# Last 16 tokens of a chunked scan as one stacked 128-row unit, and two output-gate tiles moved from the tail into the carries

## The reference

```python
def step(S, inp):
    r_t, w_t, k_t, v_t, kk_t, a_t = inp
    sa = jnp.einsum('bhvk,bhk->bhv', S, kk_t)
    S = (S * w_t[:, :, None, :]
         - sa[..., None] * (kk_t * a_t)[:, :, None, :]
         + v_t[..., None] * k_t[:, :, None, :])
    return S, jnp.einsum('bhvk,bhk->bhv', S, r_t)
...
o = ((o - mean) * lax.rsqrt(var + GN_EPS)).reshape(B, T, RWKV_WIDTH) * gn_g + gn_b
o = (o + bonus.reshape(B, T, RWKV_WIDTH)) * g
...
gate_a, gate_b = jnp.split(jax.nn.sigmoid(gate_logits), N_BRANCH, axis=-1)
h = h + (gate_a * y_a + gate_b * y_b) @ w_o[l]
```

## Time and profile before

| | us |
|---|---|
| median of 3 runs | 1664.49 (1661.36 to 1671.22) |
| profiled execution | 1663.75 |
| span of the profiled execution | 1661.8 |
| carry before the second recurrence, first F matmul to first step | 665.77 to 674.10 |
| second recurrence, first step to last matmul between the steps | 674.10 to 709.27 |
| head sums to first branch tile | 714.03 to 753.01 |

### The profile page before, as it was taken

How to read it: one execution, slowest core, us unless ns; L and a number is a source line. 1 busy time by engine, 2 the same in 40 slices (tenths; PEclk the granted TensorE clock), 3 DMA queues, 4 the chain that set the end, 5 groups by cost and what they waited for, 6 DMA issues and landing times.

```text
span 1661.8 us, 32663 instructions
## 1 busy us (share of the span) xinstructions
PE 1559.3 (94%) x11824; PEld 1420.6 (85%) x11824; DVE 1087.2 (65%) x1794; ACT 826.2 (50%) x1425; POOL 379.5 (23%) x168
## 2 busy tenths in 40 slices
PE   5998879999688989898999999999999999999998
PEld 4975569999678988788999999999999888888886
DVE  3424557777668777565549898799999544444444
ACT  3434545555355522134455566667666444444444
POOL 1210112222113200011224324322122222222222
PEclk8995899999789988689999999999999999999999
DMA  6630125556324400024545555544444466666654
GB/s 229 235 119 0 39 78 176 178 188 184 95 89 140 152 2 2 3 84 145 177 139 180 176 177 179 178 148 130 140 137 139 155 188 188 189 189 189 188 187 142
DMA packets 66233, 234.89 MB, mean 141 GB/s; under 512 B 8200, under 2 KB 9240, under 8 KB 66160
## 3 DMA queue, kind: packets, MB, share of 16 engines
q1 hardware_dynamic: 65760, 232.31, 44.9%
q0 software_dynamic: 400, 1.59, 0.3%
HBM read 232.80 MB, written 1.06 MB: 141 GB/s over the span
## 4 chain that ended last, share of the span: by engine, by line
PE 80%; issue 9%; DVE 5%; ACT 3%; POOL 2%; DMA 0%; SPq 0%; DVEq 0%; ACTq 0%; POOLq 0%
PE psum L671 40%; PE psum L1286 21%; PE psum L685 4%; PE psum L1252 3%; PE psum L996 2%; POOL w_lo L513 1%; DVE big L1546 1%; PE psum L659 1%; PE psum L1080 1%; PE psum L791 1%; PE psum L836 1%; PE psum L729 1%; PE psum L1085 1%; PE psum L809 1%; DVE big L1646 1%
## 5 line engine op out<-in xcount | busy, mean ns | idle before, releaser
L671 PE MATMUL psum<-x_hi,w_hi 128*128 128x256 f32 (+1 forms) x2192 | 634.7, 290 | 37.3 <-DVE x_lo L1341 16.5
L671 PE MATMUL psum<-x_lo,w_hi 128*128 128x256 f32 (+1 forms) x2192 | 625.0, 285 | 0.0
L671 PE MATMUL psum<-x_hi,w_lo 128*128 128x256 f32 (+1 forms) x2192 | 621.2, 283 | 0.0
L513 POOL TENSOR_TENSOR w_lo<-ring,w_hi 128x1024 fp32r<-128x1024 f32 x141 | 349.0, 2475 | 1163.7 <-ACT w_hi L499 1163.7
L499 ACT ACTIVATE w_hi<-ring 128x1024 fp32r<-128x1024 f32 x424 | 445.4, 1050 | 92.4 <-PE psum L671 80.2
L671 PEld LDWEIGHTS psum<-x_hi,w_hi 128*128 128x128 f32 x2192 | 417.9, 191 | 47.4 <-issue 31.6
L513 DVE TENSOR_TENSOR w_lo<-ring,w_hi 128x1024 fp32r<-128x1024 f32 x283 | 352.9, 1248 | 157.3 <-ACT w_hi L499 153.9
L671 PEld LDWEIGHTS psum<-x_hi,w_lo 128*128 128x128 f32 x2192 | 420.8, 192 | 0.0
L671 PEld LDWEIGHTS psum<-x_lo,w_hi 128*128 128x128 f32 x2192 | 418.9, 191 | 1.6 <-issue 1.4
L1971 DVE TENSOR_TENSOR h_lo<-big,h_hi 128x256 fp32r<-128x256 f32 x128 | 69.2, 541 | 163.1 <-ACT h_hi L2360 163.1
L1286 PE MATMUL psum<-w_hi,h_hi 128*128 128x512 f32 x512 | 160.8, 395 | 0.0
(11 more groups left out here) (284 smaller groups left out, 1763.4 us busy)
## 6 DMA issues: line engine op xcount, KB each, us to landing
ring<-experts SPq DMA_DIRECT2D x256, 512.0 KB, 3.6
ring<-w_ffn SPq DMA_DIRECT2D x66, 512.0 KB, 3.6
ring<-w_in SPq DMA_DIRECT2D x46, 512.0 KB, 3.6
ring<-w_mid SPq DMA_DIRECT2D x24, 512.0 KB, 3.6
ring<-w_out SPq DMA_DIRECT2D x16, 512.0 KB, 3.9
ring<-w_q SPq DMA_DIRECT2D x16, 512.0 KB, 4.0
big<-w_cmp SPq DMA_DIRECT2D x8, 512.0 KB, 5.6
big<-bias_rows POOLq DMA_DIRECT2D x1, 1536.0 KB, 8.5
```

What stands on the lines that cost most here:

```text
L513: eng.tensor_tensor(w_lo[:, n % RING, :], ring[:, n % RING, :], w_hi[:, n % RING, :].bitcast(F32), ALU.subtract).then_inc(low_ready2 if n ...
L671: mm = pe.matmul(dst, w[:, slot, k * P:(k + 1) * P], x[:, k, t0:t0 + width], start=(n == 0), stop=(n == 3 * len(chunks) - 1))
```

## The change

Group 2 gets code of its own. The 8 heads times 16 tokens are stacked into one block of 128 rows: the upper 64 rows hold the even heads, the lower 64 the odd ones (`side(0)`, `side(1)`), and a gram is one 64x64 matmul to a side, of which the mask keeps the blocks of one head with itself. The blocks off the two sides are zeroed once, and a product, power or application is then one 128-row matmul for all heads. Its effects stand inside the last step. ACT packs four features into `rms` before the scan. Two gate tiles, 8 and 9, are taken out of the tail: in each carry, half of a tile's matmuls follow `carry_values(0)` and half follow `carry_values(1)`. Their sigmoids go to rows of `z2` that are free by then. The splits of tiles 10 to 12 (high) and 10 (low) move into the scan, and those of the tail move up by two.

```diff
+        HOLE_BANK = (7, 5)
+        gate_row = lambda g: 12 + g if g in (8, 9) else g
-        LAST = {"turn": 6, "lt": (3, 5), "l": (3, 5), "qr": (3, 5), "mv": (7, 3), "l2": (7, 3), "l2t": (7, 3), "app0": (4, 5),
...
+        LAST = {"turn": 6, "grams": 3, "mv": 4, "l2": 5, "l2t": 7, "app0": 6, "l4": 5, "l4t": 7, "app1": 4, "l8t": 3, "app2": 6,
+                "app3": 4, "e": 5, "o": 7}
+        stack_gram = lambda a: gram[0][:, a, 0, :]
+        stack_y = ycol[0][:, 0, :]
...
+            def gate_part(g, bank, n0, n1):
+                slot = tile_split(pe, B_MID + g)
+                for n in range(n0, n1):
+                    k = n // 3
+                    w, x = ((w_hi, x_hi), (w_hi, x_lo), (w_lo, x_hi))[n % 3]
+                    mm = pe.matmul(psum[:, bank, 0:TX], w[:, slot, k * P:(k + 1) * P], x[:, k, N_META:T2],
+                                   start=(n == 0), stop=(n == 23))
+                if n1 == 24:
+                    mm.then_inc(tiles_used, 1)
...
+            def stack_grams():
+                kinds = ((S_BETA, alpha), (S_KAPPA, alpha), (S_ALPHA, beta), (S_BETA, rho), (S_KAPPA, rho))
+                for k, (a, b) in enumerate(kinds):
+                    for x in range(2):
+                        mm = pe.matmul(psum[side(x), LAST["grams"], k * HD:(k + 1) * HD], stack_in[side(x), a, :], b[side(x), :, T_LAST],
+                                       start=True, stop=True)
+                mm.then_inc(gram_sum[0], 1)
+            def stack_product(name, a, rhs):
+                return pe.matmul(psum[:, LAST[name], 0:rhs.shape[1]], stack_gram(a), rhs, start=True, stop=True)
+            def stack_first():
+                pe.wait_ge(stack_zeroed, 2)
+                pe.wait_ge(gram_ready[0], 18)
+                pe.wait_ge(tm_ready, 13)
+                stack_product("mv", G_MT, stack_v).then_inc(pow_sum[0], 1)
+                stack_product("l2", G_LT, stack_gram(G_L)).then_inc(pow_sum[0], 1)
+                stack_product("l2t", G_L, stack_gram(G_LT)).then_inc(pow_sum[0], 1)
...
                 for hh in range(2):
                     pe.wait_ge(eo_ready[hh], 2 * tg + 2)
                 carry_values(0)
+                pe.wait_ge(f_ready, 4 * tg + 4)
+                gate_part(8 + tg, HOLE_BANK[tg], 0, 12)
                 carry_values(1).then_inc(g_sum, 1)
-                pe.wait_ge(f_ready, 4 * tg + 4)
+                gate_part(8 + tg, HOLE_BANK[tg], 12, 24)
                 pe.wait_ge(g_ready, 2 * tg + 2)
                 for c in range(8):
...
+                    if tg == 0 and c == 6:
+                        pe.wait_ge(gate_sig, 1)
                     if tg == 0:
                         turn_in(1, (2 * c, 2 * c + 1))
                     elif c == 0:
-                        turn_in(2, range(8))
+                        stack_turn()
                     elif c == 1:
...
+                        stack_grams()
                     elif c == 2:
...
+                        pe.wait_ge(gate_sig, 2)
+                        stack_first()
                     elif c == 3:
-                        apply_power(2, 0, 0)
-                        second_products(2, 0)
-                        apply_power(2, 1, 0)
+                        stack_apply(0)
+                        stack_second()
                     elif c == 4:
...
+                        stack_apply(1)
+                        stack_third()
...
                     elif c == 7:
-                        apply_power(2, 1, 3)
-            effects(2, 0)
-            effects(2, 1)
-            for hh in range(2):
-                pe.wait_ge(eo_ready[hh], 6)
+                        stack_effects()
+            pe.wait_ge(eo_ready[0], 6)
             pe.wait_ge(o_ready, 2)
             recur(2, 0).then_inc(out_sum, 1)
...
-            output_gate(8, 0)
-            output_gate(9, 1)
+            output_gate(10, 0)
+            output_gate(11, 1)
...
-            for g in range(10, 16):
-                if g >= 12:
+            for g in range(12, 16):
+                if g >= 14:
                     pe.wait_ge(gate_sig, g - 11)
-                output_gate(g, g % 4)
+                output_gate(g, (g - 10) % 4)
...
+            def stack_zero():
+                for x in range(2):
+                    dve.memset(gram[0][side(x), :, 0, side(1 - x)], 0.0).then_inc(stack_zeroed, 1)
+            def stack_keep():
+                dve.wait_ge(gram_sum[0], 13)
+                for x in range(2):
+                    for k, kinds, dst, mask in ((0, 2, G_LT, "upper"), (2, 1, G_L, "lower"), (3, 2, G_QT, "upper_in")):
...
+            def stack_add(j):
...
+                dve.tensor_tensor(stack_y, psum[:, LAST[f"app{j}"], 0:P], stack_y, ALU.add).then_inc(app_ready[0], 1)
...
                     if tg == 0:
+                        if c in (3, 5):
+                            split_low(dve, B_MID + 10 + (c - 3) // 2)
                         continue
                     if c == 0:
                         conv_pair()
+                        stack_zero()
                     elif c == 1:
...
+                        stack_keep()
+                    elif 3 <= c < 7:
+                        stack_add(c - 3)
                     elif c == 7:
-                        add_power(2, 1, 3)
+                        stack_add_effects()
                 add_out(tg)
...
-            split_low(dve, B_MID + 10)
+            split_low(dve, B_MID + 12)
             dve.wait_ge(gn_root, 1)
             dve.reciprocal(gn_s[:, 0, :], gn_s[:, 0, :]).then_inc(gn_formed, 1)
-            split_low(dve, B_MID + 11)
+            split_low(dve, B_MID + 13)
...
-            split_low(dve, B_MID + 12)
-            split_low(dve, B_MID + 13)
+            split_low(dve, B_MID + 14)
...
-            split_low(dve, B_MID + 14)
+            split_low(dve, B_MID + 15)
             step(dve.tensor_tensor(gn_d, gn_d, bonus, ALU.add))
-            split_low(dve, B_MID + 15)
...
+            for n, src in enumerate((alpha, z2[:, 16:20, 1:T2 + 1], beta, kappa)):
+                act.activation(stack_in[:, n, :].rearrange("p (m t) -> p m t", m=4), src[:, :, 2 * P:T2], ACT.Copy).then_inc(stack_packed, 1)
...
+                gate_out(8 + tg, HOLE_BANK[tg])
+                if tg == 0:
+                    split_high(act, B_MID + 10)
+                    split_high(act, B_MID + 11)
+                else:
+                    split_high(act, B_MID + 12)
...
-            for g in range(8, 16):
-                if g >= 10:
+            for g in range(10, 16):
+                if g >= 12:
                     split_high(act, B_MID + g + 2)
...
+                gate_out(g, (g - 10) % 4)
```

More of the change, by code:

```diff
@@ L1087, in recur, with stack_turn @@
                 return mm
+            T_LAST = slice(2 * P, T2)
+            S_ALPHA, S_V, S_BETA, S_KAPPA = range(4)
+            def stack_turn():
+                pe.wait_ge(stack_packed, 4)
+                for n, src in enumerate((S_ALPHA, S_V)):
+                    for x in range(2):
+                        mm = pe.matmul(psum[side(x), LAST["turn"], n * HD:(n + 1) * HD], stack_in[side(x), src, :],
+                                       const("ident")[side(x), side(x)], start=True, stop=True)
+                    mm.then_inc(tm_sum, 1)
@@ new lines, in stack_effects @@
+            def stack_effects():
+                pe.wait_ge(app_ready[0], 12)
+                for x in range(2):
+                    pe.matmul(psum[side(x), LAST["e"], 0:HD], stack_y[:, 0:HD], stack_gram(G_QT)[:, side(x)], start=True, stop=True)
+                    pe.matmul(psum[side(x), LAST["o"], 0:HD], stack_v, stack_gram(G_RT)[:, side(x)], start=True, stop=False)
+                    mm = pe.matmul(psum[side(x), LAST["o"], 0:HD], stack_y[:, HD:P], stack_gram(G_QT)[:, side(x)], start=False, stop=True)
+                mm.then_inc(eo_sum[0], 1)
@@ L2205, in _, with gate_out @@
                 act.activation(gate_z[:, g, :], psum[:, (22 + g) % 4, 0:TX], ACT.Sigmoid).then_inc(in2_copied, 1)
+            def gate_out(g, bank):
+                act.wait_ge(tiles_used, B_MID + g + 1)
+                act.activation(z2[:, gate_row(g), 1:TX + 1], psum[:, bank, 0:TX], ACT.Sigmoid).then_inc(gate_sig, 1)
             def copy_power(tg, hh, name, k, dst):
```

163 lines of the change are left out of this document (81 added, 82 removed).

## The result

The changed kernel takes 1641.86 us (median of 4 runs, 1634.13 to 1646.22) against 1667.86 for the kernel before, measured beside it (4 runs, 1661.36 to 1671.33). The ratio is 0.9855, 95% interval 0.9816 to 0.9894: faster, by 18 to 31 us. The forecast was 1642.0. The number is right; several of its terms are not, and their errors cancel. The profiled execution took 1642.6 us with a span of 1640.8, against 1663.75 and 1661.8.

The account below looks back on a forecast made before the run. PE was taken as the bound, busy 94% of the span, with the second recurrence at 1.2 GHz. Terms -15.5 - 4.2 + 0.8 + 0.1 - 3.3 = -22.1 gave 1641.7 us profiled, 1642 median; range 1631 to 1653.

Parts of the forecast that it names:

- Term 1 and 2: Second recurrence and end of the scan: stacked unit saves 13.2 us, effects inside the last step 2.3; together 15.5.
- rival B: Single chain shows: PE waits 4 us in c2 to c7, carries keep 3.4 of issue stall; 1648 to 1653; chance 0.18.
- rival D: Stacked matmuls issued as small ones or paying for their 128-wide weights apart: 8 us given back, 1650; chance 0.06.
- Term 3: Tail: two gate tiles fewer are 5.8 us, of which 4.2 come through because of DVE's splits.
- The moves "at nothing": Splits of tiles 10 to 12 moved into the scan on ACT, DVE and POOL, costed at nothing.
- Term 4: Gate tiles in the carries: first carry 0.8 us worse, second costs 0, with PE's instruction supply catching up.
- 1.7 stays in the path, in each carry: Carries: term 4's other case, where instruction supply does not catch up and the issue hole of 1.7 us remains.
- Term 5: Clock in the recurrences: filled holes hold 2.4 GHz for about 3.5 us, gaining 2.8 in the first, 0.5 in the second.
- rival A: The clock holds: filled holes keep 2.4 GHz through both recurrences, 15.2 us from the clock; 1629; chance 0.14.
- signs of being wrong: Stacked products waiting over 2 us, a 1.5 to 1.7 us hole left beside the gate, or the recurrence holding 2.4 GHz.
- Term 1's packing copies: Four packing copies on ACT before the first group, in its idle time: 0 to 0.3 us, taken as 0.1.
- Rival C: Slower than before: low clock lasts through the tail's gate tiles and three branch tiles, 27 us more, 1669; chance 0.03.

Follow-up runs that it names:

- e3: Changed kernel with POOL's low part of tile 11 held back until the second recurrence is over; 1629.15 us, in the repeat 1628.07 us.
- e7: Changed kernel with tile 11's low part held back, both decay products made on ACT, and DVE's taps and memsets reordered; 1624.69 us, ratio 0.9758.
- e8: Same as e7, but with gate tiles 8 and 9 back in the tail; 1637.32 us, ratio 0.9852.
- e4: Changed kernel with each carry's gate tile placed whole behind the second values instead of half before them; 1640.94 us, ratio 0.9884.
- e2: Kernel before plus only the two gate tiles in the carries and their moved splits, last 16 tokens as before; 1656.41 us, ratio 0.9958.

## Why the prediction was right, and where it was not

- **Term 1 and 2, -15.5: right.** Alone the stack gave 14.7 and 15.2. A record with 128 moving columns costs 1.58/6 = 0.26 (681.79 to 683.37), where I took 0.23, so the steps with products are 0.2 longer than priced (3.40 against 3.21). The end of the scan took 696.88 - 694.47 = 2.4 (2.5). The memsets took 0.43 each and the six keeps 1.27 (0.5 and 1.2). Between the stacked products PE waited 0.3 us in all, so rival B's first half and rival D are refuted: PE covers each result at the low clock, and at the high clock too (17.0 in e3), apart from the 0.3 for the masked grams and the 1.42 for `add_state(1)`. This wait the prediction had priced at nothing under the low clock's cover; at the high clock the cover is gone.
- **Term 3, -4.2: right (-4.4),** and by its own steps: the extra split of 1.16 ahead of the spread, the fourth tile behind DVE's split of tile 15. DVE's gains came at 1.41 instead of 3.50, and the product ahead of them paid 1.6 more.
- **The moves "at nothing": wrong, +4.0.** The step that failed is "POOL gets to 11 after its second decay product ... I cost these at nothing". POOL's 2.56 us beside DVE's taps made PE wait 3.43 instead of 1.05, and the clock fell in that wait, which made the products 1.63 longer (11.15 against 9.52): 4.0 together. In the table it stands as +2.4 since the grams ahead of it were 1.6 shorter by the clock (5.93 against 7.54). I had looked at POOL's queue and at who waits for its result, but not at what its instructions do to the engine beside it. The trace of before could have told: four taps take 1.73 there, so twelve should take 5.2, and beside POOL's decay product they took 8.41.
- **Term 4, +0.8 and 0: wrong, +2.2 and +2.1.** The step that failed is "I take it that PE's supply of instructions catches up behind the long gate matmuls". With the gate's 2.92 us the carries lost only 0.7 and 0.9 us of their holes. In the first carry 0.84 us of issue was left, of the 1.4 that the sum lacks; in the second 1.0 ahead of the gate and 0.72 behind it, of 2.1. The rest is in the lengths of the values and the half tiles. The prediction had kept the other case as "1.7 stays in the path, in each carry", and that was nearer.
- **Term 5, -3.3: wrong, -9.3 in the first recurrence and the grams behind it.** The choice that failed was the nearest row. I took the 3.5 us at 679.5 as the measure of how long a filled hole holds the clock. It holds through all eight steps, 12.5 us, in all ten profiled executions that have a gate tile in the first carry, and in none of the four that haven't. That the tile in the first carry decides is shown, by e7 against e8 above all, and its place within the carry doesn't matter (e4). In the second recurrence the clock does fall, after 6.5 to 7.1 us, in the change's three executions and in e2, and in e3 to e7 it holds to within half a microsecond of either end. For the changed kernel the row I took (3.5 us) was short by half there, and what decides isn't shown. It isn't the tile alone: in e3_again and e4 to e7 the clock fell in the second carry in spite of the tile, for 3 to 7 us, and was back for the recurrence, and e8, without a tile, ran only the first 5.8 us of it at 1.2 GHz. So rival A was half true of the changed kernel. Its condition came true in e3, where it asks for 35.8 us less than before and the medians gave 32.2 and 35.9; but e3 is another kernel, and that its 1629.15 and 1628.07 meet rival A's 1629 is in part chance. Of the prediction's own signs of being wrong, the last came ("if the recurrence holds 2.4 GHz"), for the first recurrence. The Trainium skill ("TensorE: Matmul & The Clock Gate", What's actually happening) says that activity releases the throttle; here the first recurrence goes with it, and the second one of the changed kernel, without a gap in PE from 680 on, does not.
- **Term 1's packing copies, +0.1:** the stretch that holds them takes 32.2 in both; nothing can be told.
- Rival C, the low clock through the tail, did not come: it returned in the same place as before.

The sum of the errors: the clock gave 6.5 more than foretold, the carries took 3.5 more and POOL's split 4.0, together 1.0 of the 1.1 between -22.1 and -21.0. The median of 1642 is right by the luck of this cancellation, not by the terms.

## What to carry to other kernels

A hole ahead of a stretch of small matmuls can cost twice, once in itself and once in the clock of what follows, so a filler there can be worth more than its own length (7.7 us of clock in the first recurrence for one tile of 2.9; ahead of the second recurrence no such rule came out of the runs). Work that is moved off the critical path onto POOL must be looked at beside DVE as well as beside its consumers: with two inputs in SBUF it stopped DVE's taps for about 0.9 us per us here. An order made for a filler has to be looked at again when the filler goes (e8). And when a change makes PE faster, price each neighbour's work again at the faster pace: 1.42 us that was hidden at 1.2 GHz showed at 2.4. A hole that a profile calls issue may be a wait all the same: compare its end with the ends of the instructions whose semaphores the code waits on there.

## What the runs showed of the hardware

- VectorE's taps beside POOL: 5.03, 8.41 and 10.52 us beside 0, 3.76 and 6.32 us of POOL's two-input work, as above. The Trainium skill ("GPSIMD Engine Reference", Specifications) has POOL share them with VectorE, with contention where a VectorE instruction has two SBUF inputs. The trace agrees for the taps, and gives the size: nearly the whole of POOL's time.
- PE's clock can be lost by a single wait of 3.43 us (0.50 at 649.5 to 651.5) and kept through one of 1.3; in the second recurrence, with the same code in it, it fell in the changed kernel and held in e3 and e4, and what decides stays open.
- A stretch of 32-row matmuls with 64 columns has holes of 0.4 to 2.3 us that no other engine explains, while a block of instructions of 16 KB lands every 3.5 to 4 us. That the blocks are the cause isn't shown.
